# One score product per level for both directions in the third mixer, with the conditioning jobs set anew

## The reference, cut to what matters

```python
def step(S, blk):
    qc, kc, vc, gc = blk
    b = jnp.cumsum(gc, axis=2)
    diff = b[:, :, :, None, :] - b[:, :, None, :, :]
    pair_decay = jnp.where(causal[:, :, None], jnp.exp(jnp.minimum(diff, 0.0)), 0.0)
    att = jnp.einsum('bhtd,bhsd,bhtsd->bhts', qc, kc, pair_decay)
    o = jnp.einsum('bhtd,bhdv->bhtv', qc * jnp.exp(b), S) + jnp.einsum('bhts,bhsv->bhtv', att, vc)
```

## Time and profile before

| | us |
|---|---|
| three runs | 1746.31, 1746.48, 1747.27 |
| median | 1746.48 |
| the profiled execution, its own time | 1743.03 |
| its span | 1740.9 |

### The profile page before, as it was taken

The page is one execution under the profiler, slowest core; times in us unless marked ns, Lnnn a source line. Parts: engine busy times, 40 slices in busy tenths (PEclk is TensorE's granted clock), DMA queues, the critical chain, the costliest instruction groups (busy, mean ns, idle before and its releaser), DMA issues. The chain is left out here.

```text
span 1740.9 us, 29515 instructions
## 1 busy us (share of the span) xinstructions
PE 1595.0 (92%) x12140; PEld 1267.4 (73%) x12140; DVE 1089.4 (63%) x1870; ACT 636.7 (37%) x1060; POOL 75.5 (4%) x112
## 2 busy tenths in 40 slices
PE   6999999878889999999999979999977799899997
PEld 4766776655678778888888867677764587678885
DVE  2287347887786674554453364745678867578776
ACT  4255222333531245222222252433243431366662
POOL 0000011200101000000000000000020100000000
PEclk8999999978999999999999989999978899999998
DMA  9411111077301034222223022112225101255551
GB/s 391 149 49 50 49 61 52 22 250 247 136 3 51 26 146 154 104 96 92 102 84 119 1 87 86 61 49 85 74 86 178 68 3 51 77 212 197 186 203 47
DMA packets 41622, 182.02 MB, mean 105 GB/s; under 512 B 4753, under 2 KB 5521, under 8 KB 33681
## 3 DMA queue, kind: packets, MB, share of 16 engines
q1 hardware_dynamic: 41488, 180.14, 29.0%
HBM read 179.08 MB, written 1.05 MB: 103 GB/s over the span
## 5 line engine op out<-in xcount | busy, mean ns | idle before, releaser
L235 PE MATMUL ps<-hr_in,wr_in 128*128 128x512 f32 (+1 forms) x544 | 221.8, 408 | 14.4 <-DVE wr_in L228 13.9
L236 PE MATMUL ps<-hr_in,wr_in 128*128 128x512 f32 (+1 forms) x544 | 209.1, 384 | 0.0
L237 PE MATMUL ps<-hr_in,wr_in 128*128 128x512 f32 (+1 forms) x544 | 208.5, 383 | 0.0
L235 PEld LDWEIGHTS ps<-hr_in,wr_in 128*128 128x128 f32 x544 | 108.4, 199 | 63.9 <-issue 35.4
L228 DVE TENSOR_TENSOR wr_in<-mix,wr_in 128x1024 fp32r<-128x1024 f32 x68 | 83.8, 1234 | 93.5 <-ACT wr_in L224 89.6
L235 PE MATMUL ps<-mix_r,work_r 128*128 128x512 f32 (+1 forms) x352 | 133.8, 380 | 1.6 <-DVE work_r L228 1.6
L236 PE MATMUL ps<-work_r 128*128 128x512 f32 (+1 forms) x356 | 135.1, 379 | 0.0
L228 DVE TENSOR_TENSOR work_r<-pr,work_r 128x2048 fp32r<-128x2048 f32 x38 | 86.9, 2288 | 67.7 <-ACT work_r L224 63.6
L237 PE MATMUL ps<-mix_r,work_r 128*128 128x512 f32 x320 | 124.5, 389 | 0.0
L237 PEld LDWEIGHTS ps<-hr_in,wr_in 128*128 128x128 f32 x544 | 108.3, 199 | 19.6
L236 PEld LDWEIGHTS ps<-hr_in,wr_in 128*128 128x128 f32 x544 | 108.8, 200 | 15.5 <-issue 0.2
(11 more groups left out here) (525 smaller groups left out, 3312.1 us busy)
## 6 DMA issues: line engine op xcount, KB each, us to landing
mix<-in_w_in SPq DMA_DIRECT2D x68, 512.0 KB, 3.7
pr<-in_w_up SPq DMA_DIRECT2D x28, 1024.0 KB, 4.9
pr<-in_ada_w SPq DMA_DIRECT2D x40, 512.0 KB, 6.3
ring<-in_w_up SPq DMA_DIRECT2D x16, 1024.0 KB, 4.8
ring<-in_ada_w SPq DMA_DIRECT2D x28, 512.0 KB, 4.5
pr<-in_w_down SPq DMA_DIRECT2D x14, 1024.0 KB, 5.0
pr<-in_ada_w SPq DMA_DIRECT2D x8, 1024.0 KB, 15.6
work<-in_w_out SPq DMA_DIRECT2D x16, 512.0 KB, 4.1
```

What stands on the lines that cost most here:

```text
L235: nc.tensor.matmul(out, sh, mh, start=first, stop=False)
L236: nc.tensor.matmul(out, sh, ml, start=False, stop=False)
L237: return nc.tensor.matmul(out, sl, mh, start=False, stop=last)
```

## The change

- A step is now one level for both directions. Keys of the forward direction fill the first half of each block, those of the backward direction the second half; queries the other way round; so one product of all 128 x 128 pairs holds both directions' scores of that level, each on its side of the diagonal. `at` holds both directions in one tensor of 2048 columns (layer 0).
- A first step without a level (`None`) takes the diagonal: the two directions' keys added, times the bare queries, multiplied by the identity mask into `at`, all of its columns. So nothing clears `at` beforehand. There are 8 steps: None, 0 to 4, 6, 5.
- The masked copies take all 512 columns of a bank, with a mask for both sides of the diagonal. Those of level 6 are plain copies on ACT (`collect_whole`), 4 of 64 rows x 256 columns a pair of banks and direction, 16 in layer 0 and 8 in layer 1.
- Level 0 copies the keys (their factor is 1) instead of an exponential and a product; its differences are taken on half of the columns.
- The key differences on DVE go; ACT's exponential takes the end sum as its bias, 8 calls of 128 columns for each direction instead of one of 1024.
- The read-out has half of its `at` products.
- Jobs: one behind each step's scores (`HIDDEN_AT`), 8 in layer 0, 6 in layer 1; the first half of a gate is spread ahead of the next scores. Jobs (1, 2), (1, 3) move from layer 0's list to its `LAST` pair, and (1, 6), (1, 7) from there to layer 1's list. Parts of the last job are in the tail.
- The gate's bias is loaded once for each gate; the far side is computed first, from the near side's copy.

The diff, cut to its core:

```diff
-LAST = (((1, 6), (1, 7)), ((1, 8), (1, 9)))
-HIDDEN = (((0, 8), (0, 4), (0, 9), (0, 5), (1, 0), (0, 10), (1, 1), (0, 11), (1, 2), (1, 3)),
-          ((1, 4), (1, 5), (1, 10), (1, 11)))
+LAST = (((1, 2), (1, 3)), ((1, 8), (1, 9)))
+HIDDEN = (((0, 8), (0, 4), (0, 9), (0, 5), (1, 0), (0, 10), (1, 1), (0, 11)),
+          ((1, 6), (1, 7), (1, 4), (1, 5), (1, 10), (1, 11)))
+HIDDEN_AT = (range(8), (0, 1, 2, 4, 5, 6))
...
-    steps = [(d, l) for l in range(LEVELS) for d in range(2)]
+    steps = (None, *range(LEVELS - 2), LEVELS - 1, LEVELS - 2)
+    WHOLE = 6
...
-    REST_AT, KEYS_AT, STATES_AT, QUERIES_AT = (0, 1), (2, 3), 8, (9, 10)
-    TURN_AT, PRODUCTS_AT, JOBS_AT = (3, 5), 7, 1
-    UNIT_AT = (11, 12)
-    KEYS_EXP_AT, QUERIES_EXP_AT, ENDS_EXP_AT, KEYS_OUT_AT = (1, 2), (4, 6), 3, (5, 7)
+    KEYS_AT, STATES_AT, QUERIES_AT = (2, 3), 6, (4, 5)
+    TURN_AT, PRODUCTS_AT = (3, 4), 5
+    UNIT_AT = (6, 7)
+    KEYS_EXP_AT, QUERIES_EXP_AT, ENDS_EXP_AT, KEYS_OUT_AT = (1, 2), (3, 4), 3, (4, 5)
...
+    def parts_at(n):
+        if n not in HIDDEN_AT[layer]:
+            return (), ()
+        q = HIDDEN_AT[layer].index(n)
+        return range(begins[q - 1] + 1 if q else 0, begins[q]), range(begins[q], begins[q] + 1)
+
+    late = range(begins[-1] + 1, PLACES)
...
-                        for side in sides(layer):
-                            sp.dma_start(gate_of(E, layer, which, side), A["gate_b"][layer, which]).then_inc(S("gate_b"), 16)
+                        sp.dma_start(gate_of(E, layer, which, sides(layer)[0]), A["gate_b"][layer, which]).then_inc(S("gate_b"), 16)
...
-            for n, (d, l) in enumerate(steps):
+            for n in range(len(steps)):
+                ahead, behind = parts_at(n)
+                for p in ahead:
+                    job(p)
                 pe.wait_ge(S("kf"), n + 1)
+                moving = queries[n % 2] if n else tiles(pr, T_HQ, 2)
...
-                if n == JOBS_AT:
-                    job(0)
-                if n < len(steps) - 2:
-                    for p in places(n):
-                        job(p)
+                for p in behind:
+                    job(p)
...
-            nc.gpsimd.memset(at[:, :], 0.0).then_inc(S("at0"), 1)
...
             def exponents(n):
-                nc.vector.tensor_tensor(dv, cv, cv[:, :, :, ref:ref + 1].to_broadcast(list(cv.shape)),
-                                        ALU.subtract).then_inc(S("dv"), 1)
+                l = steps[n]
+                for d in range(2):
+                    cv, dv = blocks(tiles(cum, 2 * d, 2), l), blocks(tiles(expo[n % 2], 2 * d, 2), l)
+                    ref = (1 << l) - 1 if d == 0 else 1 << l
+                    if l == 0:
+                        ins = nc.vector.tensor_tensor(dv[:, :, :, 1 - d:2 - d], cv[:, :, :, 1 - d:2 - d], cv[:, :, :, d:d + 1], ALU.subtract)
+                    else:
+                        ins = nc.vector.tensor_tensor(dv, cv, cv[:, :, :, ref:ref + 1].to_broadcast(list(cv.shape)), ALU.subtract)
+                ins.then_inc(S("dv"), 1)
...
             def factors(n):
+                l, k = steps[n], keys[n % 2]
+                if n == 0:
+                    nc.vector.tensor_tensor(two(k, layer), two(keys_of(0), layer), two(keys_of(1), layer), ALU.add).then_inc(S("kf"), 1)
+                    return
+                if l == 0:
+                    for d in range(2):
+                        nc.vector.tensor_copy(half(k, l, d == 1), half(keys_of(d), l, d == 1))
+                dve.wait_ge(S("exps"), n)
+                if l:
+                    for d in range(2):
+                        nc.vector.tensor_tensor(half(k, l, d == 1), half(k, l, d == 1), half(keys_of(d), l, d == 1), ALU.mult)
+                nc.vector.tensor_tensor(two(queries[n % 2], layer), two(queries[n % 2], layer), two(tiles(pr, T_HQ, 2), layer), ALU.mult)\
+                    .then_inc(S("kf"), 1)
...
             def collect(n):
+                l, done = steps[n], n - (n > WHOLE)
+                if n == WHOLE + 1:
+                    dve.wait_ge(S("at_whole"), 2 * len(pairs))
...
+                        if n == 0:
+                            ins = nc.vector.tensor_tensor(dst, src, mask.rearrange("p (b t) -> p b t", b=1).to_broadcast([P, 4, P]), ALU.mult)
+                        else:
+                            ins = nc.vector.copy_predicated(dst, mask.bitcast(I32).rearrange("p (b t) -> p b t", b=1).to_broadcast([P, 4, P]), src)
+                        ins.then_inc(S("at"), 1)
...
+            for n in range(1, len(steps)):
+                ahead, behind = parts_at(n)
                 factors(n)
                 if n + 2 < len(steps):
                     exponents(n + 2)
-                if n >= 1:
+                for p in ahead or behind:
+                    spread_out(p)
+                if n - 1 != WHOLE:
                     collect(n - 1)
...
+                for p in (*(behind if ahead else ()), *(late[:1] if n == len(steps) - 1 else ())):
+                    spread_out(p)
...
             def exps(n):
+                act.wait_ge(S("dv"), n)
                 if n >= 2:
                     act.wait_ge(S("s_mm"), len(pairs) * (n - 1))
+                for d in range(2):
+                    sooner, later = d == 1, d == 0
+                    e = tiles(expo[n % 2], 2 * d, 2)
+                    if l:
+                        nc.scalar.activation(half(k, l, sooner), half(e, l, sooner), ACT.Exp, scale=-1.0)
+                    ins = nc.scalar.activation(half(q_, l, later), half(e, l, later), ACT.Exp)
+                ins.then_inc(S("exps"), 1)
+
+            def collect_whole():
+                act.wait_ge(S("at"), 2 * len(pairs) * WHOLE)
+                for m, jj in enumerate(pairs):
+                    act.wait_ge(S("s_mm"), len(pairs) * WHOLE + m + 1)
+                    for q in range(2):
+                        for d in range(2):
+                            rows_, part = (slice(0, P // 2), slice(P // 2, P)) if d == 0 else (slice(P // 2, P), slice(0, P // 2))
+                            dst = at[rows_, jj[0] * 512:jj[0] * 512 + 1024].rearrange("p (b q t) -> p b q t", b=4, q=2)[:, :, q, part]
+                            ins = nc.scalar.copy(dst, score_bank(WHOLE, m, q)[rows_, :].rearrange("p (b t) -> p b t", b=4)[:, :, part])
+                        ins.then_inc(S("at_whole"), 1)
...
+                for p in (*ahead, *behind):
+                    row_out(p)
+                if n == WHOLE:
+                    collect_whole()
...
-                for p in places(n) if n < len(steps) - 2 else late[:1] if n == len(steps) - 2 else ():
+                for p in late[:1] if n == len(steps) - 1 else ():
                     row_out(p)
```

More of the change, by code:

```diff
@@ L1834, in states @@
                 ins.then_inc(S("kv_out"), 1)
-            exponents(0)
+            factors(0)
             exponents(1)
-            for n in range(len(steps)):
+            exponents(2)
+            for n in range(1, len(steps)):
+                ahead, behind = parts_at(n)
                 factors(n)
@@ L1953, in _ @@
                     r = KEYS_EXP_AT.index(n)
-                    act.wait_ge(S("rest"), r + 1)
-                    nc.scalar.activation(tiles(kd, 2 * r, 2), tiles(kd, 2 * r, 2), ACT.Exp).then_inc(S("kd_exp"), 1)
+                    for b in range(2 * TILES):
+                        cv = tiles(cum, 2 * r, 2)[:, b * P:(b + 1) * P]
+                        ins = nc.scalar.activation(tiles(kd, 2 * r, 2)[:, b * P:(b + 1) * P], cv, ACT.Exp, bias=cv[:, end(r):end(r) + 1], scale=-1.0)
+                    ins.then_inc(S("kd_exp"), 1)
                 if n == ENDS_EXP_AT:
```

104 lines of the change are left out of this document (32 added, 72 removed).

## The result

The kernel after takes **1737.44 us** (median of four, 1735.91 to 1739.83), the kernel before 1746.88 in the same comparison (four, 1746.31 to 1750.11). The ratio is 0.9943, 95% interval 0.9926 to 0.9961: faster by 9.4 us, where 22 were forecast, and 0.4 us above the range. The profiled execution took 1735.91 us around a span of 1734.1.

The account below looks back on a forecast made before the run. The stage was taken as set by DVE's work plus delays that jobs bring into PE's order. Layer 0 18.3, tail 2, layer 1 3.5, less 2 for the clock: 22 us, from 1746.48 to 1724.5 us; range 1715 to 1737.

Parts of the forecast that it names:

- The DVE sum: DVE's work in layer 0's steps falls from 76.3 to 63.3 us; by that ratio layer 1's from 45.5 to 37.7.
- The product records: Sign to look for: 384 score records instead of 672 in each of PE and its loads.
- The path was the one named: End of layer 0's loop: job 7's last quarter lands 7.9 us after job 6 frees a slot, blocks end at 414.9.
- With a gate addition instead of a coefficient 8.0: Layer 0, from ACT's last row copy to the tail's first scan: 8.0 us, against 7.5 before.
- the walk: Step-by-step timing of jobs and engines through both layers: scan 18.3 us earlier in layer 0, 3.5 in layer 1.
- about the same clock: Granted clock in both loops stays about as before; 2 us taken off for PE steps walked at full clock.
- The tail: Layer 0 behind the scan: fewer read-out products, no job blocks before the second low-rank product, fewer DVE waits; 2 us saved.
- Following PE's order quarter by quarter I get 1340: Layer 1: transfers lead; six jobs and the biases from 1296 us end at 1340, the scan 3.5 us earlier.
- (b): Rival, low clock: PE at 0.5 through layer 0, layer 1 some 3 us longer; 9 us gained, 1737; chance 0.08.
- Rival (a): Both loops: only DVE's work comes back, idle time stays, longer layer 0 end costs 7; 14 us gained, 1732; chance 0.17.
- (c): Rival, slower: in gate steps PE and DVE run one behind the other at low clock; 20 us slower, 1766; chance 0.04.
- (d): Rival, faster: layer 1's weights stream at 5.7 us a job and ACT's path overlaps; 29 us gained, 1717.5; chance 0.12.

Follow-up runs that it names:

- d1_dve: Kernel after, with level 6 collected by DVE as the other levels are and nothing on ACT; 1736.90 us, ratio 0.9953 to the kernel before.
- w1_warm: Kernel after, with four needless 128x512 products on PE around the end of layer 0's loop; 1735.81 us, ratio 0.9944 to the kernel before.
- l1_four: Kernel after without jobs (1,6) and (1,7) in layer 1, their coefficients set to zero; 1720.69 us, ratio 0.9862 to the kernel before.
- t1_small: Kernel after, with two of layer 1's six jobs loading 16 columns of 1024 per quarter, engines' work kept; 1733.85 us, ratio 0.9945.
- f1_free: Kernel after, with each layer's last job's blocks behind the first read-out and its spreads later, all work done; 1721.73 us, ratio 0.9867.
- a1_order: Kernel after, with ACT's table load and three activations ahead of the last job's row copy in layer 0; 1736.01 us, ratio 0.9954.

## Why the prediction was wrong

**The DVE sum was right within 1.4 us.** 63.3 us were forecast for layer 0 and 61.9 measured; 37.7 for layer 1 and 37.7 measured. The product records are the 384 that were named. The copies of 64 rows were miscounted, in the list of the change too: 12 in the trace (8 and 4) and not 24 (16 and 8), at 366 ns each as in the earlier trace rows; d1_dve shows that nothing hung on this. The two level-0 copies of layer 0 took 0.67 us from the start of the first to the next operation, not the 1.20 taken.

**Layer 0, the loop: right within 3 us.** The last row copy was forecast 67.5 us after the start and came at 69.1, 70.2, 70.5 and 67.8, 1.9 later in the mean. The path was the one named: the last two quarters were issued from 411.28 us and PE made their blocks at 417.84 and 419.11, some 7.8 us after.

**Layer 0, from that copy to the scan: the first term that failed.** "With a gate addition instead of a coefficient 8.0" took a path at the upper clock from the earlier trace rows: the granted clock was 1.00 in before's tail and is 0.50 over the same path in the kernel after, and it took 10.8 us. w1_warm gives the 8.0 back, so the clock is the cause. The clock fell while PE stood for the last job's last quarters, a wait that the walk itself had named; it priced the path behind it as if the clock stayed up. The walk had put "about the same clock" and 2 us for all of it.

**The tail: 2 us were forecast, 0.2 to 0.8 came.** From the scan to the end of the stage it was 23.0 us before and is 22.2 to 22.8 in four profiles. In w1_warm it is 20.5: the forecast saving is there, and the low clock eats it. 2 of the loop, 2.8 to the scan, 1.5 in the tail, and 1.3 by which the profile of before that the walk began from was longer than the mean of two: these make up the 7.6 us by which layer 0 fell short (20.3 forecast, 12.7 measured).

**Layer 1: the step that failed most.** "Following PE's order quarter by quarter I get 1340", that is 44.3 us after the start, took a job at a pace between 5.7 and 7.9 us. In four profiles with this code the last row copy came at 47.9, 51.5, 50.0 and 50.4, mean 50.0. The six row copies of after lie 8.1, 7.7, 6.9, 6.7 and 8.5 us apart, 7.6 in the mean: near the slow end of the bounds. l1_four shows the cause and its size: with four jobs the gain is 9.7 us, more than DVE's own saving, and the two added jobs take 12.9 back, where the walk had left 3.5 us of gain. t1_small splits the price about evenly between the transfers and the jobs' work in PE's order. From the row copy to the scan it took 7.5 us in the mean where 6.7 were put. The forecast was 3.5 us faster; it came 3.2 slower.

So 20.3 - 12.7 = 7.6 us are missing in layer 0 and 3.5 + 3.2 = 6.7 in layer 1; less the 2 us allowed for the clock these are 12.3, the way from the forecast sum (21.8, rounded to 22) to 9.5.

**The rivals.** The time fell on that of (b), but not for its reason: the loop of layer 0 ran at a granted clock of 0.85 and not at 0.5, and the clock's price came behind the last job, on the way to the scan and in the tail. The rule of the Trainium skill ("TensorE: Matmul & The Clock Gate", section on HAM oscillation), that bursts with waits for data between them start slow again, agrees with these rows, at that place: the blocks at 417.84 us ran at 1.00 and those behind the next wait for weights at 0.5. Its consequence was sought in the loops. Where PE waited for DVE in them a fall is seen too (the clock is 0.50 from 379 to 381 and from 396 to 398 us), in two steps of the kernel after:

```profile
377.81 3.45 PE L1681 MATMUL ps<-ring,work 64*128 64x128 f32 x32 [2.51 <-DVE work L1829]
386.89 2.06 PE L1681 MATMUL ps<-ring,work 64*128 64x128 f32 x32
395.46 3.58 PE L1681 MATMUL ps<-ring,work 64*128 64x128 f32 x32 [2.77 <-DVE work L1829]
```

The step that didn't wait takes 2.06 us. These waits are for the collection two steps back, since the scores have two pairs of banks until the states are out. They were not foreseen and cost little, as the loop came out within 3 us. Rival (a), only DVE's work back, comes near in the loop of layer 0, where DVE has 14.4 us less to do and the loop is 14.0 shorter; but its reason, PE and DVE waiting in turn, is not what the trace shows, since 10.5 of DVE's 15.1 us of idle time there are the one wait for the last job. In layer 1 its 8 us did not come at all. (c) did not happen. (d), weights at 5.7 us a job, is refuted by the row copies.

**The range.** Its upper end was (b)'s 1737. It stood for one unfavourable term at a time; here the low clock of the tail and the price of two more jobs in layer 1 came together. What stays open is which part of layer 1's other half (the blocks ahead of scores, or the clock after the waits that they cause) costs how much: no run parts them. It stays open too which waits PE's clock can bear: in f1_free it fell to 0.57 in the stretch from 410 us behind a wait of only 0.72 us.

## What to carry to other kernels

When work is halved in a loop that also hides transfers or side jobs, price the hidden jobs again at the new length: here two jobs cost 3.8 to 5.4 us in the long loops and 10 to 13 in the short ones, and moving them from one loop to the other mostly moved that price. Look at what is queued last in the loop on the waiting engine; taking each layer's last conditioning job off the path to the scan was worth more (17 us) than the whole change (7 to 9.4). And when a step of a path comes behind waits of PE that did not exist before, cost it at the lower clock too, and look in the profile at where the clock fell: here it was ahead of the longest wait, not in it.

## What the runs showed of the hardware

Equal code scatters more than had been assumed: the 1550 us outside the two stages took from 1551.2 to 1568.5 us in fourteen profiles, and the kernel before from 1735.4 to 1754.0 in 80 executions of the four comparisons above. A part of it may be the clock. In the kernel after, some 3 us of the first stretch (341 to 344 us, granted clock 0.50) ran like this, behind a wait for DVE, and then at the upper level again:

```profile
340.14 1.51 PE L1164 MATMUL ps<-const,pr 128*128 128x128 f32 x8 [1.91 <-DVE pr L1332]
342.30 0.63 PE L238 MATMUL ps<-hr_in,wr_in 128*128 128x512 f32 x1
344.51 0.39 PE L238 MATMUL ps<-hr_in,wr_in 128*128 128x512 f32 x1
```

The granted clock of that first stretch was 0.94 to 0.97 over the profiles, its length 346.4 to 352.2 us. That the clock is all of the scatter is not shown.

A copy of 128x512 from SBUF to SBUF took DVE 0.42 us by its record (0.34 from start to start), where an operation with two inputs of that size takes 0.69 (0.60). And PE's clock fell behind waits for weights of 1.84 and 0.63 us (after) and of 1.16 and 0.46 us (a1_order): while it was 0.50, the four low-rank products took 3.78 us and not 1.98, whether the 3.67 us of waiting stood ahead of them (after) or not (a1_order).
